# Turning attention probabilities on VectorE and through DRAM instead of on TensorE

## The chip, the cores and the metric

One core of a Trainium2 chip runs the whole kernel. The metric is the device time in microseconds (us), the median of several runs. The engines named below are TensorE (PE), VectorE (DVE), ScalarE (ACT), GpSimd (Pool) and SyncE (SP), which issues most of the transfers; sixteen DMA engines carry them out.

## What is computed

One layer of an encoder block on 512 tokens of width 2048, in float32:

```python
proj = rms_norm(h, g) @ w_in                       # q, k, v of both mixers
att_a = chunk_band_attention(q_a, k_a, v_a, 1, bias_a, sinks)   # 16 heads, 4 key heads, ALiBi
att_b = chunk_band_attention(q_b, k_b, v_b, 8, rel_bias, None)  # 16 heads, relative bias
gates = sigmoid(xn @ w_gate)
h = h + (gates[:D] * (att_a @ w_branch_a) + gates[D:] * (att_b @ w_branch_b)) @ w_out
h = h + square(relu(rms_norm(h, g2) @ w_mlp_in)) @ w_mlp_out
out = rms_norm(h, g3)
```

with, for each head, `p = softmax(q @ k.T / 8 + bias)` and `o = p @ v`. In mixer A a chunk of 64 tokens sees itself and the chunk before it; in mixer B it sees itself and up to eight chunks before it, which for 512 tokens is every chunk up to its own.

## The kernel before

Every product is split into a high and a low part: a matrix is copied by ACT to a float32r tile (`w_hi`, `xn_hi`, `pt_hi`), DVE subtracts that from the original (`w_lo`, `xn_lo`, `pt_lo`), and PE multiplies high by high, high by low and low by high.

The part that matters here is the first stage. It makes 22 blocks of 256 columns (q, k, v and the first gates, `BLOCKS`), each from four units; a unit is a 128 x 1024 piece of weights that SP loads into one of four slots of `landing` (L494), that ACT and DVE split (L686, L1032), and that PE multiplies with 24 matmuls (L1707 to L1709). SP loads unit n when the low part of unit n - 4 is made. There are 88 units, numbered 0 to 87, and the 32 heads of both mixers are hung between them by three lists, written out by hand:

```python
SCORES_AT = [13 + 2 * k for k in range(16)] + [46, 48, 51, 53, 56, 59, 62, 65, 68, 71, 74, 76, 78, 81, 83, 85]
TURN_AT = [n + 1 for n in SCORES_AT]
PV_AT = [n + 2 for n in SCORES_AT]
PV_AT[28] = 81
```

So the scores of a head stand behind unit m on PE (`scores`, L1782), the turning of its probabilities behind unit m + 1 (`turn_probs`, L1796), and the product with the values behind unit m + 2 (`times_v`, L1817). ACT and DVE run the same lists two units later in their own order: in their pass for unit n they handle what hangs on unit n - 2. In such a pass DVE adds the bias and takes the maximum (L1131), splits the unit (L1032), makes the low part of a turned head (L1169), adds up an output (L1145), normalises (L1160), and scales or splits a finished block (L1082 to L1115). ACT splits the unit (L686), copies an output half (L770), takes the exponentials (L751), copies a turned head to `pt_hi` (L761), evacuates a block (L727 to L731 or the gate's sigmoid, L714) and, for the next head, doubles its q (L742, four instructions), for which the next scores wait.

`turn_probs` turns 128 x 128 blocks with a matmul by the identity, from `probs` in SBUF to the PSUM banks that held the scores: 7 blocks for a head of mixer A, 10 for one of B, 272 in all. The scores of the next head therefore wait until DVE has read them.

Beside this, Pool runs `totals` (L1642, L1645): 18 rounds that sum blocks of the two MLP matrices in DRAM for a fast matrix product at the end, each with four copies and four accumulating transfers of 1 MB, DRAM to DRAM, in a chain of waits. Round m starts when PE has used 12 + 8m units (for m up to 9), so round 9 waits for 84 units. Their results are wanted only much later.

Of the kernel before, what the change touches and what calls it, by code (L numbers as in the profile page):

```python
# [13 lines left out]
P = 128  # L14
# [121 lines left out]
def bank_end(h, t):  # L136

    tiles = head_tiles(h)
    return max(i for i in range(TT) if tiles[i][2] == tiles[t][2]) + 1
# [6 lines left out]
def build(nc, x, w_in, a_sinks, b_rel_bias, w_branch_a, w_branch_b, w_gate, w_out,  # L146
          norm_final_g, x_features, norm_gains, identity_in, alibi_in, up_units, x_turned, up_ends, down_blocks, out):
    rel_rows = nc.dram_tensor("rel_rows", (B_HEADS, REL_ROW), F32, kind="Internal").ap()
    h_rows = nc.dram_tensor("h_rows", (SEQ, D), F32, kind="Internal").ap()
    hidden_rows = nc.dram_tensor("hidden_rows", (CHUNKS, 4, P, 4, CB), F32, kind="Internal").ap()  # L150
# [14 lines left out]
    with ExitStack() as ctx:  # L165
# [36 lines left out]

        first_phase = ExitStack()
# [5 lines left out]
        pt_hi = sb("pt_hi", [P, TT, 512], F32R, first_phase)  # L209
        pt_lo = sb("pt_lo", [P, TT, 512], F32R, first_phase)  # L210
# [119 lines left out]
        def turned_part(part, h, t):  # L330

            if h >= A_HEADS:
                return part[:, t, 0:P * (t + 1)]
            if t == 0:
                return part[:, 0:1, 0:P]
            at = 512 * (t - 1) + P
            return part[:].rearrange("p t n -> p (t n)")[:, at:at + 768].rearrange("p (b n) -> p b n", n=384)[:, :, 0:P]
# [58 lines left out]
        pt_done = sem("pt_done")  # L396
# [90 lines left out]
        def _(sp):  # L487
# [32 lines left out]
            for c, (kind, mixer, i) in enumerate(BLOCKS):  # L520
# [4 lines left out]
                for u in range(KU):  # L525
# [26 lines left out]
                    if n - 6 in SCORES_AT and SCORES_AT.index(n - 6) + 2 < HEADS:  # L552
                        strip(SCORES_AT.index(n - 6) + 2)
                    n += 1

# [124 lines left out]
        def _(act):  # L680
# [74 lines left out]
            def turned_probs(h):  # L755
                for t, (first, n, bk, col, _) in enumerate(head_tiles(h)):
                    act.wait_ge(pt_done, TT * h + bank_end(h, t))
                    turned = bank[:, bk, col:col + turned_keys(h, t)]
                    if h < A_HEADS:
                        turned = turned.rearrange("p (b n) -> p b n", n=P)  # L760
                    nc.scalar.activation(turned_part(pt_hi, h, t), turned, ACT.Copy)\  # L761
                        .then_inc(pt_hi_done, 1)
# [10 lines left out]
            def stage(n):  # L773
# [5 lines left out]
                if n in TURN_AT:  # L779
                    turned_probs(TURN_AT.index(n))  # L780
# [22 lines left out]
            for t in range(TT):  # L803
                if t != 2:
                    split(1, (0, 1, None, 2)[t])
                act.wait_ge(rows_landed[t], 16)
                for g in (0, 1):
                    if t >= 2:
                        act.wait_ge(squared, 2 * t + g - 3)
                    nc.scalar.activation(pt_hi[:, (2 * t + g) % 4, :], x_rows[:, t, g * QC:(g + 1) * QC], ACT.Square,  # L810
                                         accum_out=squares[:, t, g:g + 1]).then_inc(squared, 1)
# [207 lines left out]
        def _(dve):  # L1019
# [97 lines left out]
            def biased_scores(h):  # L1117
# [8 lines left out]
                if h:  # L1126
                    dve.wait_ge(pt_done, TT * h)
# [35 lines left out]
            def turned_probs(h):  # L1163
                for t, (first, n, bk, col, _) in enumerate(head_tiles(h)):
                    dve.wait_ge(pt_hi_done, TT * h + bank_end(h, t))
                    turned = bank[:, bk, col:col + turned_keys(h, t)]
                    if h < A_HEADS:
                        turned = turned.rearrange("p (b n) -> p b n", n=P)
                    nc.vector.tensor_tensor(turned_part(pt_lo, h, t), turned, turned_part(pt_hi, h, t).bitcast(F32),  # L1169
                                            ALU.subtract)\  # L1170
                        .then_inc(pt_lo_done, 1)
# [47 lines left out]
            for n in range(2 * KU, UNITS1 + 1):  # L1219
# [7 lines left out]
                if m in TURN_AT:  # L1227
                    turned_probs(TURN_AT.index(m))
# [383 lines left out]
        def _(pool):  # L1612
# [54 lines left out]
            for m in range(2 + STEPS):  # L1667
                pool.wait_ge(unit_used, 12 + 8 * m if m < 10 else 84 + 10 * (m - 9))
# [35 lines left out]
        def _(pe):  # L1704
# [82 lines left out]
            def turn_probs(h):  # L1787
                if h == 0:
                    pe.wait_ge(const_landed, 16)
                    pe.wait_ge(unseen_zero, 1)  # L1790
                for t, (_, n, bk, col, at) in enumerate(head_tiles(h)):
                    pe.wait_ge(probs_ready, TT * h + t + 1)
                    keys = turned_keys(h, t)
                    start = at + n - keys
                    for k in range(keys // P):
                        ins = nc.tensor.transpose(bank[:, bk, col + k * P:col + (k + 1) * P],  # L1796
                                                  probs[:, start + k * P:start + (k + 1) * P], identity[:])
                    ins.then_inc(pt_done, 1)

            def times_v(h):  # L1800
# [5 lines left out]
                pe.wait_ge(pt_lo_done, TT * (h + 1))  # L1806
                if h:
                    pe.wait_ge(att_ready, h)
                for j in range(TT):
# [192 lines left out]
```

## Time and profile before

| | |
|---|---|
| median of 3 runs | 2479.81 us (2479.39 to 2479.84) |
| the profiled execution | 2479.84 us |
| its span in the trace | 2477.9 us |
| PE / DVE / ACT / Pool busy | 99% / 67% / 43% / 8% of the span |
| TensorE clock granted | full, in all 40 slices |
| first stage (units 0 to 87) | to 598.8 us of the span |

The page divides the span into 40 slices of 62 us; slices 2 to 10 are the stage of the change. Matmuls overlap in the records (a 128 x 512 one takes 0.39 us and the next starts 0.23 us after it), so what a piece of PE's work is worth is read from the chain of work that ended last, where overlaps are taken out, and not from the busy time of its group.

### The profile page before, as it was taken

The page shows a single profiled execution, that of the slowest core. Times are in us where ns is not written, and L with a number is a line of the kernel's source. Part 1 is how long each engine was busy: PE and PEld are TensorE (multiplying, and loading weights), DVE is VectorE, ACT ScalarE, POOL GpSimd, SP SyncE. Part 2 cuts the span into 40 slices and gives each one's busy share as a digit, 9 for nine tenths or more (in the row PEclk, how much of TensorE's full clock was granted, in tenths as well). Part 3 has the DMA queues.
Part 4 walks back from the last instruction along what each step waited for, and adds up shares of the span by engine and source line. Part 5 has one row for each costly group of instructions (what it writes and reads, how often), then busy time and mean ns, then how long its engine had stood idle before and what let it go on. Part 6 is the DMA issues. An engine that isn't in the chain of part 4 may idle for free.

```text
span 2477.9 us, 34645 instructions
## 1 busy us (share of the span) xinstructions
PE 2460.3 (99%) x14162; PEld 2176.5 (88%) x14162; DVE 1658.9 (67%) x2252; ACT 1062.5 (43%) x1381; POOL 193.2 (8%) x185
## 2 busy tenths in 40 slices
PE   9999999999999999999999999999999999999998
PEld 8898898898888888888999999999998888888886
DVE  6566555556333332544788888888869788877897
ACT  5566755556222222312433433333335444444445
POOL 0010100100010100001200000000001011110010
PEclk9999999999999999999999999999999999999999
DMA  7789998898889999964564433334478666566652
GB/s 261 208 236 261 240 246 243 233 253 225 227 241 271 245 254 254 251 184 151 167 192 152 136 129 132 133 128 132 133 233 332 232 230 226 190 224 231 233 191 107
DMA packets 226818, 517.10 MB, mean 209 GB/s; under 512 B 30672, under 2 KB 159840, under 8 KB 215152
## 3 DMA queue, kind: packets, MB, share of 16 engines
q1 hardware_dynamic: 213856, 364.04, 44.3%
q0 software_dynamic: 12672, 151.00, 24.1%
q8 instruction: 103, 1.69, 0.3%
q14 instruction: 43, 0.35, 0.0%
q10 hardware_dynamic: 144, 0.02, 0.0%
HBM read 489.80 MB, written 176.20 MB: 269 GB/s over the span
## 4 chain that ended last, share of the span: by engine, by line
PE 96%; DVE 2%; ACT 1%; DMA 0%; issue 0%; SPq 0%; DVEq 0%; ACTq 0%
PE bank L1707 31%; PE bank L1709 31%; PE bank L1708 31%; PE bank L1782 1%; PE bank L1817 1%; PE bank L1796 1%; DMA stream<-in_x_features 0%; DVE up_lo L1398 0%; DVE form_lo_b L1364 0%; DVE at_lo L1248 0%; ACT q_twice L742 0%; DVE ring L1506 0%; ACT w_hi L686 0%; ACT L714 0%; DVE raw_forms L1469 0%
## 5 line engine op out<-in xcount | busy, mean ns | idle before, releaser
L1032 DVE TENSOR_TENSOR w_lo<-landing,w_hi 128x1024 fp32r<-128x1024 f32 x199 | 247.6, 1244 | 447.2 <-ACT w_hi L686 447.1
L1707 PE MATMUL bank<-xn_hi,w_hi 128*128 128x512 f32 x1184 | 464.7, 392 | 2.3 <-DVE w_lo L1189 1.4
L1709 PE MATMUL bank<-xn_hi,w_lo 128*128 128x512 f32 x1184 | 461.2, 390 | 0.0
L1708 PE MATMUL bank<-xn_lo,w_hi 128*128 128x512 f32 x1184 | 460.8, 389 | 0.0
L686 ACT ACTIVATE w_hi<-landing 128x1024 fp32r<-128x1024 f32 x199 | 210.9, 1060 | 575.6 <-PE bank L1709 575.2
L909 ACT ACTIVATE up_hi<-up_raw 128x1792 fp32r<-128x1792 f32 x128 | 218.1, 1704 | 401.8 <-PE bank L1709 395.0
L958 ACT ACTIVATE ring<-down_raw 128x1024 fp32r<-128x1024 f32 x224 | 237.5, 1061 | 312.4 <-PE bank L1709 312.4
L1506 DVE TENSOR_TENSOR ring<-down_raw,ring 128x1024 fp32r<-128x1024 f32 x224 | 284.9, 1281 | 68.3 <-ACT ring L958 68.2
L1398 DVE TENSOR_TENSOR up_lo<-up_raw,up_hi 128x1792 fp32r<-128x1792 f32 x128 | 259.8, 2030 | 85.8 <-ACT up_hi L909 85.8
L1707 PEld LDWEIGHTS bank<-xn_hi,w_hi 128*128 128x128 f32 x1184 | 222.4, 188 | 47.3 <-issue 3.3
L1709 PEld LDWEIGHTS bank<-xn_hi,w_lo 128*128 128x128 f32 x1184 | 222.2, 188 | 46.9
L1708 PEld LDWEIGHTS bank<-xn_lo,w_hi 128*128 128x128 f32 x1184 | 222.5, 188 | 45.0 <-issue 0.2
L1707 PE MATMUL bank<-ring,down_forms 128*128 128x512 f32 x656 | 255.5, 390 | 0.9 <-DVE ring L1506 0.9
L1708 PE MATMUL bank<-ring,down_forms 128*128 128x512 f32 x656 | 255.3, 389 | 0.0
L1709 PE MATMUL bank<-ring,down_forms 128*128 128x512 f32 x656 | 255.2, 389 | 0.0
L1707 PE MATMUL bank<-form_hi_b,up_hi 128*128 128x256 f32 x896 | 253.8, 283 | 0.4 <-DVE up_lo L1398 0.4
L1707 PE MATMUL bank<-form_hi_a,up_hi 128*128 128x256 f32 x896 | 253.6, 283 | 0.0
L1708 PE MATMUL bank<-form_lo_b,up_hi 128*128 128x256 f32 x896 | 253.6, 283 | 0.0
L1709 PE MATMUL bank<-form_hi_b,up_lo 128*128 128x256 f32 x896 | 253.6, 283 | 0.0
L1708 PE MATMUL bank<-form_lo_a,up_hi 128*128 128x256 f32 x896 | 253.6, 283 | 0.0
L1709 PE MATMUL bank<-form_hi_a,up_lo 128*128 128x256 f32 x896 | 253.6, 283 | 0.0
L1707 PEld LDWEIGHTS bank<-form_hi_b,up_hi 128*128 128x128 f32 x896 | 172.0, 192 | 0.7 <-DVE up_lo L1398 0.6
(192 smaller groups left out, 4384.1 us busy)
## 6 DMA issues: line engine op xcount, KB each, us to landing
down_totals<-in_down_blocks POOLq DMA_DIRECT2D x64, 1024.0 KB, 9.5
up_raw<-in_up_units SPq DMA_DIRECT2D x128, 512.0 KB, 3.4
down_raw<-down_totals SPq DMA_DIRECT2D x128, 512.0 KB, 4.4
down_raw<-in_down_blocks SPq DMA_DIRECT2D x96, 512.0 KB, 4.3
landing<-in_w_in SPq DMA_DIRECT2D x71, 512.0 KB, 6.5
landing<-in_w_gate SPq DMA_DIRECT2D x64, 512.0 KB, 6.5
landing<-in_w_out SPq DMA_DIRECT2D x32, 512.0 KB, 3.7
hidden_rows<-hidden_out SPq DMA_DIRECT2D x32, 512.0 KB, 3.3
```

What stands on the lines that cost most here:

```text
L686: nc.scalar.activation(w_hi[:, u % SPLIT, :], landing[:, u % LAND, :], ACT.Copy).then_inc(unit_hi, 1)
L909: nc.scalar.activation(up_hi[n % 2], up_raw[n % 3][:, 1:8, :], ACT.Copy).then_inc(up_hi_done, 1)
L958: nc.scalar.activation(ring[i % RING][:, 0, :], raw_of(i), ACT.Copy).then_inc(piece_hi, 1)
L1032: nc.vector.tensor_tensor(w_lo[:, s, :], landing[:, u % LAND, :], w_hi[:, s, :].bitcast(F32), ALU.subtract).then_inc(unit_lo, 1)
L1398: nc.vector.tensor_tensor(up_lo[n % 2], up_raw[n % 3][:, 1:8, :], up_hi[n % 2].bitcast(F32), ALU.subtract).then_inc(up_lo_done, 1)
L1506: nc.vector.tensor_tensor(part[:, 1, :], raw_of(i), part[:, 0, :].bitcast(F32), ALU.subtract)\
L1707: nc.tensor.matmul(dst, a_hi, b_hi, start=start, stop=False, **kw)
L1708: nc.tensor.matmul(dst, a_hi, b_lo, start=False, stop=False, **kw)
L1709: return nc.tensor.matmul(dst, a_lo, b_hi, start=False, stop=stop, **kw)
L1782: ins = nc.tensor.matmul(bank[:, bk, col:col + n], query[:, t * P:(t + 1) * P], keys[:, first:first + n], start=col == 0 and k == 0, stop= ...
L1796: ins = nc.tensor.transpose(bank[:, bk, col + k * P:col + (k + 1) * P], probs[:, start + k * P:start + (k + 1) * P], identity[:])
L1817: ins = nc.tensor.matmul(dst, v_parts[:, s, j, head, :], moving, start=j == 0 and part is pt_hi, stop=j == TT - 1 and part is pt_lo, skip_ ...
```

## The change

The turning leaves PE. When a head is normalised, DVE turns each of its 128 x 128 blocks in one instruction that transposes the sixteen 32 x 32 blocks each within its own 32 partitions, into a new tile `probs_by_block`. SP stores that tile to DRAM (`turned_probs`, two places in turn) and reads it back with four transfers of 32 partitions each, which put the 32 x 32 blocks on the partitions where they belong (`pt_raw`). ACT and DVE then make `pt_hi` and `pt_lo` from `pt_raw`, each in one instruction per head in place of four. `times_v` reads them in the new order, and for mixer A multiplies whole blocks (256 columns in place of 192). The turned copy is now taken behind unit m + 3 and the values behind unit m + 4. The last head's two are one unit earlier, and its store and loads are issued by Pool, ahead of the wait of round 9. Scores wait for the head before to be biased only.

```diff
-SCORES_AT = [13 + 2 * k for k in range(16)] + [46, 48, 51, 53, 56, 59, 62, 65, 68, 71, 74, 76, 78, 81, 83, 85]
-TURN_AT = [n + 1 for n in SCORES_AT]
-PV_AT = [n + 2 for n in SCORES_AT]
-PV_AT[28] = 81
+SCORES_AT = [13 + 2 * k for k in range(16)] + [46, 48, 51, 53, 56, 59, 62, 65, 68, 71, 74, 76, 78, 80, 82, 84]
+TURN_AT = [n + 3 for n in SCORES_AT[:-1]] + [SCORES_AT[-1] + 2]
+PV_AT = [n + 4 for n in SCORES_AT[:-1]] + [SCORES_AT[-1] + 3]
...
+        def store_probs(queue, h, out):
+            queue.wait_ge(probs_turned, h + 1)
+            if h >= 2:
+                queue.wait_ge(turned_back, 64 * (h - 1))
+            size = turned_size(h)
+            queue.dma_start(turned_probs[h % 2, :, 0:size], probs_by_block[:, 0:size]).then_inc(out, 16)
+        def load_probs(queue, h, out, landed, back):
+            queue.wait_ge(out, landed)
+            if h:
+                queue.wait_ge(pv_done, h)
+            size = turned_size(h)
+            for r in range(4):
+                rows = slice(32 * r, 32 * (r + 1))
+                cols = slice(r * size // 4, (r + 1) * size // 4)
+                src = turned_probs[h % 2, :, cols].rearrange("(a c) n -> c a n", c=32)
+                queue.dma_start(pt_raw[rows, 0:size].rearrange("p (a n) -> p a n", a=4), src)\
+                    .then_inc(back, 16)
...  (SP, behind the load of unit n)
+                    if n - 6 in SCORES_AT:
+                        store_probs(sp, SCORES_AT.index(n - 6), turned_out)
+                    if n - 7 in SCORES_AT:
+                        h = SCORES_AT.index(n - 7)
+                        load_probs(sp, h, turned_out, 16 * (h + 1), turned_back)
...  (DVE)
+            def turn_probs(h):
+                dve.wait_ge(probs_ready, TT * (h + 1))
+                if h == 0:
+                    dve.wait_ge(unseen_zero, 1)
+                else:
+                    dve.wait_ge(turned_out, 16 * h)
+                ...
+                for k, (t, j) in enumerate(blocks):
+                    ...
+                    ins = nc.vector.transpose(out[:, k], probs[:, start:start + P])
+                ins.then_inc(probs_turned, 1)
...
                 if head is not None:
                     normalise(head)
+                    turn_probs(head)
...  (Pool)
             for m in range(2 + STEPS):
+                if m == 9:
+                    store_probs(pool, HEADS - 1, last_out)
+                    load_probs(pool, HEADS - 1, last_out, 16, last_back)
                 pool.wait_ge(unit_used, 12 + 8 * m if m < 10 else 84 + 10 * (m - 9))
...  (PE, scores)
-                    pe.wait_ge(pt_lo_done, TT * h)
+                    pe.wait_ge(biased, TT * h)
```

A head of mixer A moves 128 x 896 floats (0.459 MB) each way, one of B 128 x 1280 (0.655 MB).

## Rows read from the trace of the kernel before

**Rows 1.** The page, part 1: busy time, share of the span, instructions.

```profile
PE 2460.3 (99%) x14162; PEld 2176.5 (88%) x14162; DVE 1658.9 (67%) x2252; ACT 1062.5 (43%) x1381; POOL 193.2 (8%) x185
```

**Rows 2.** Waits of PE from 0 to 1000 us (total, times, longest): the longest.

```profile
PE bank L1707 <- DVE w_lo L1189: 1.4, 1, 1.4
```

**Rows 3.** Chain that ended last, mixer A: start us, us, what.

```profile
94.89 0.77 PE bank L1796 x7
...
101.14 0.84 PE bank L1817 x8
101.98 0.92 PE bank L1782 x8
...
108.38 0.77 PE bank L1796 x7
```

**Rows 4.** The same chain near the end of mixer B.

```profile
561.77 1.19 PE bank L1796 x10
568.42 1.21 PE bank L1817 x8
569.63 1.33 PE bank L1782 x8
```

**Rows 5.** Timeline of DVE, a head of A: start, us, instruction.

```profile
198.83 0.29 DVE L1131 CUSTOM_DVE_ANT_0 probs<-bank,strips 128x128 f32<-128x128 f32 x1 [3.38 <-issue]
...
202.72 0.97 DVE L1160 TENSOR_SCALAR probs<-probs,row_inv 128x128 f32<-128x128 f32 x4
```

**Rows 6.** Timeline of ACT, mixer A: doubling of q, evacuation of a q block.

```profile
206.33 1.27 ACT L742 ACTIVATE q_twice<-q_hi 64x512 fp32r<-64x512 f32 x2
...
220.04 1.92 ACT L731 ACTIVATE q_hi<-side 64x2048 fp32r<-64x2048 f32 x1
```

**Rows 7.** Timelines of DVE and of ACT, a head of B.

```profile
571.10 0.29 DVE L1131 CUSTOM_DVE_ANT_0 probs<-bank,strips 128x128 f32<-128x128 f32 x1 [5.25 <-issue]
...
575.61 1.27 DVE L1160 TENSOR_SCALAR probs<-probs,row_inv 128x128 f32<-128x128 f32 x4
...
575.18 0.19 ACT L751 ACTIVATION_READ_ACCUMULATOR probs<-probs,neg_max 128x1 f32 x1
```

**Rows 8.** Timeline of DVE, a later stage: transposes in blocks of 32 x 32.

```profile
1234.25 1.30 DVE L1344 STREAM_TRANSPOSE mix<-stream 128x512 f32<-128x512 f32 x2
```

**Rows 9.** The page, part 5: splits of 1024 columns on DVE and ACT.

```profile
L1032 DVE TENSOR_TENSOR w_lo<-landing,w_hi 128x1024 fp32r<-128x1024 f32 x199 | 247.6, 1244 | 447.2 <-ACT w_hi L686 447.1
...
L686 ACT ACTIVATE w_hi<-landing 128x1024 fp32r<-128x1024 f32 x199 | 210.9, 1060 | 575.6 <-PE bank L1709 575.2
```

**Rows 10.** Landings of transfers from 90 to 600 us: KB each, median us.

```profile
landing<-in_w_in SPq DMA_DIRECT2D x53, 512.0 KB, 6.4
...
strips<-rel_rows SPq DMA_DIRECT2D x16, 256.0 KB, 7.6
```

**Rows 11.** The same of a later stage: a store to DRAM by 32 partitions.

```profile
h_rows<-turned_ahead SPq DMA_DIRECT2D x24, 128.0 KB, 3.6
```

**Rows 12.** Window: busy PE, PEld, DVE, ACT, POOL, PEclk, DMA share, GB/s.

```profile
78.00:569.00 491.00, 490.37 (x2839) 431.66 (x2838) 288.17 (x719) 303.23 (x629) 49.12 (x73) 1.00 0.90 243
```

**Rows 13.** DMA queues from 78 to 569 us: packets, MB, share of 16 engines.

```profile
q0 software_dynamic: 6334, 75.50, 60.2%
q1 hardware_dynamic: 41850, 43.31, 29.0%
```

**Rows 14.** The same from 0 to 78 us, before Pool moves anything.

```profile
q1 hardware_dynamic: 12352, 17.71, 66.2%
```

**Rows 15.** Waits of Pool from 60 to 600 us for units used by PE.

```profile
POOL down_totals L1642 <- PE bank L1709: 47.8, 8, 8.4
```

**Rows 16.** Timeline of Pool: last transfer of round 8, start of round 9.

```profile
559.46 0.81 POOL L1645 DMA_DIRECT2D down_totals<-in_down_blocks  x1 [4.91 <-DMA down_totals<-down_totals]
568.72 1.02 POOL L1642 DMA_DIRECT2D down_totals<-in_down_blocks  x2 [8.45 <-PE bank L1709]
```

**Rows 17.** Timeline of PE: values of the last head, end of the stage.

```profile
597.56 0.39 PE L1817 MATMUL bank<-pt_hi,v_parts 128*128 128x512 f32 x1
```

More of the change, by code:

```diff
@@ L133, in turned_keys, with turned_blocks @@
     return P * (1 + (t > 0)) if h < A_HEADS else P * (t + 1)
-def bank_end(h, t):
-    tiles = head_tiles(h)
-    return max(i for i in range(TT) if tiles[i][2] == tiles[t][2]) + 1
+def turned_blocks(h):
+    if h < A_HEADS:
+        return [(t, j) for j in range(TT) for t in (j, j + 1) if t < TT]
+    return [(t, j) for j in range(TT) for t in range(j, TT)]
 PV_BANK = 7
@@ L208, in build @@
         v_parts = sb("v_parts", [P, 2, TT, 4, 2 * DH], F32R, first_phase)
-        pt_hi = sb("pt_hi", [P, TT, 512], F32R, first_phase)
-        pt_lo = sb("pt_lo", [P, TT, 512], F32R, first_phase)
+        pt_hi = sb("pt_hi", [P, PROBS], F32R, first_phase)
+        pt_lo = sb("pt_lo", [P, PROBS], F32R, first_phase)
+        probs_by_block = sb("probs_by_block", [P, PROBS], F32, first_phase)
         probs = sb("probs", [P, PROBS], F32, first_phase)
@@ L753, in exponentials, with turned_high @@
                         .then_inc(exp_done, 1)
[L755 to L762, printed above, removed]
+            def turned_high(h):
+                if h < HEADS - 1:
+                    act.wait_ge(turned_back, 64 * (h + 1))
+                else:
+                    act.wait_ge(last_back, 64)
+                size = turned_size(h)
+                nc.scalar.activation(pt_hi[:, 0:size], pt_raw[:, 0:size], ACT.Copy).then_inc(pt_hi_done, 1)
             def attended(h):
@@ L807, in _ @@
                 for g in (0, 1):
-                    if t >= 2:
-                        act.wait_ge(squared, 2 * t + g - 3)
-                    nc.scalar.activation(pt_hi[:, (2 * t + g) % 4, :], x_rows[:, t, g * QC:(g + 1) * QC], ACT.Square,
+                    if t >= 1:
+                        act.wait_ge(squared, 2 * t + g - 1)
+                    nc.scalar.activation(pt_hi[:, g * QC:(g + 1) * QC], x_rows[:, t, g * QC:(g + 1) * QC], ACT.Square,
                                          accum_out=squares[:, t, g:g + 1]).then_inc(squared, 1)
@@ L1161, in normalise, with turned_low @@
                                             ALU.mult).then_inc(probs_ready, 1)
[L1163 to L1171, printed above, removed]
+            def turn_probs(h):
+                dve.wait_ge(probs_ready, TT * (h + 1))
+                if h == 0:
+                    dve.wait_ge(unseen_zero, 1)
+                else:
+                    dve.wait_ge(turned_out, 16 * h)
+                blocks = turned_blocks(h)
+                out = probs_by_block[:, 0:turned_size(h)].rearrange("p (r b j) -> p b r j", r=4, j=32)
+                for k, (t, j) in enumerate(blocks):
+                    _, n, _, _, at = head_tiles(h)[t]
+                    start = at + n - turned_keys(h, t) + P * (j if h >= A_HEADS else j - max(t - 1, 0))
+                    ins = nc.vector.transpose(out[:, k], probs[:, start:start + P])
+                ins.then_inc(probs_turned, 1)
+            def turned_low(h):
+                dve.wait_ge(pt_hi_done, h + 1)
+                size = turned_size(h)
+                nc.vector.tensor_tensor(pt_lo[:, 0:size], pt_raw[:, 0:size], pt_hi[:, 0:size].bitcast(F32),
+                                        ALU.subtract).then_inc(pt_lo_done, 1)
             nc.vector.memset(ones, 1.0).then_inc(ones_ready, 1)
@@ L1785, in scores @@
                 ins.then_inc(scores_done, 1)
[L1787 to L1798, printed above, removed]
             def times_v(h):
```

45 lines of the change are left out of this document (25 added, 20 removed).

## The prediction

> **What bounds the kernel now.** I read the page first: PE is busy 99% of the span [rows 1]. Then the waits of PE: over the first 1000 us, where the whole change lies, the longest is 1.4 us [rows 2] and all five kinds together are 5.2 us. So nothing but PE's own work sets the time, and any instruction taken from PE is worth its full length as long as nothing becomes late. The next question is what has room. DVE is busy 288 of 491 us in the stage of the change, ACT 303, but the DMA engines 0.90 of the time [rows 12]. That is the resource to watch: the queues' table gives 60.2% of the sixteen engines to Pool's sums in DRAM and 29.0% to SP's loads [rows 13]. Pool waits for PE only 47.8 us in eight rounds [rows 15], 6 us a round; the rest of the time it is in its chain of transfers.
>
> **What PE loses.** In the chain that ended last the seven turnings of a head of A are 0.77 us, the ten of one of B 1.19 us [rows 3, 4]. 16 x 0.77 + 16 x 1.19 = 31.4 us go. `times_v` of A has 256 columns in place of 192 in six of eight matmuls; in B eight matmuls with 512 to 128 columns take 1.21 us, in A eight of 192 and 128 take 0.84 [rows 3, 4], so it grows by well under 0.1 a head; I take 0.5 us in all. The moving operand is now read in runs of 32 elements. No row shows such a read; bounds are nothing and a doubling of `times_v` (16 x 0.84 + 16 x 1.21 = 33 us). I take nothing, since B's reads in runs of 128 columns cost 1.21 us for 2560 columns, 0.47 ns each, against 5.48 us for the 12288 of a unit, 0.45 ns each. That the scores now wait for `biased` alone gains nothing, as PE did not wait there. The sum without new waits: 2479.8 - 31.4 + 0.5 = 2449 us.
>
> **What DVE and ACT get.** Two transposes of 128 x 512 take 1.30 us [rows 8], 0.16 us per 128 columns if only columns count; the smallest DVE instruction of 128 columns takes 0.29 [rows 5]. I take 0.29: 2.0 us for a head of A, 2.9 for B, 79 us in all, so DVE goes to about 75% of the stage. `pt_hi` and `pt_lo` become one instruction each, by the 1024-column rows [rows 9] 0.93 and 1.09 us in A (896 columns), 1.3 and 1.55 in B (1280), somewhat less than before. Queued behind the turning on DVE is the split of the next unit. In A normalising ends 4.9 us after the scores [rows 5], the turning 6.9; with a q block's scaling (2.8 us) the split would end at 10.9, and PE wants it 11.0 after (two units of 5.5, from the end of one turning to the next values [rows 3]). Its cover is just enough; if it is gone it costs tenths, in some six places.
>
> **What the transfers cost one by one.** A load of 512 KB takes 6.4 us in this stage, one of 256 KB 7.6 [rows 10]; the nearest store, in a quieter stage, 3.6 [rows 11]. Store and read-back follow each other, and the four reads are issued one after another (about 0.5 us each, 1.5 more). So D, from the turning's end to the data back, is 6.4 + 1.5 + 6.4 = 14.3 us, with bounds 8.7 (3.6 twice) and 16.7 (7.6 twice). Three places want it sooner:
> - In B, nine heads have the next scores three units on. There DVE's and ACT's passes take the bias and exponentials of head h + 1 ahead of the turned copy of head h. A loop closes: turning of h, D, `pt_hi` 1.3, `pt_lo` 1.55, normalising h + 1 (1.27 and 0.2), turning h + 1 (2.9): 7.2 + D = 21.5, against a period of 3 x 5.5 + 1.21 + 1.33 = 19.0 [rows 4]. 2.5 x 9 = 23 us. Even with D short, the exponentials end 4.3 us after the scores of h + 1 [rows 7], then come 1.3 and 1.55: 7.2 against one unit of 5.5, so 1.6 x 9 = 14 us at least.
> - In A, ACT must copy the head, often evacuate a block (1.92) and double q (2 x 1.27) [rows 6] before the scores after next: 6.9 + 14.3 + 0.93 + 1.92 + 2.54 = 26.6 against 2 x (11.0 + 0.84 + 0.92) - 0.92 = 24.6: 2 us for each of the eight heads with an evacuation, 16 us.
> - The last heads of B, two units apart: 5.8 + 2.9 + 14.3 + 2.9 = 25.9 against 24.5, of which each head bears half: 4 us.
> Together some 43 us, which alone would give 2449 + 43 = 2492. SP is blocked meanwhile at its read-back, for the store and for the values of the head before; queued behind it are the loads of units, which have four units (22 us) of lead and cover it. DVE's own new wait, for the store of the head before, has 12.7 us in A and more in B, against one landing of 6.4 to 7.6; behind it stands the split of the next unit. Behind ACT's wait for the read-back stand the evacuation and the doubling priced above.
>
> **What the transfers cost together.** This decides. Up to the last head Pool has to finish rounds 0 to 8, for the last head's store stands on Pool's queue in front of round 9, behind a 1 MB transfer of round 8. Before, that transfer was issued at 559.5 and Pool then waited until 568.7 [rows 16]. The engines' time up to there, from 78 us on: 0.602 x 491 = 296 us for Pool, 0.290 x 491 = 142 for SP, 2 for the rest, 440 of 491. The 31 heads before the last add 2 x (16 x 0.459 + 15 x 0.655) = 34.3 MB. One MB of SP's queue takes 142 / 43.31 = 3.3 us beside Pool, and alone 0.662 x 78 / 17.71 = 2.9 us [rows 13, 14]: 100 to 113 us more. I take 100, since packets are longer in the stores. No row excludes that part of it fits between Pool's packets; the bound on that side is nothing. 440 + 100 = 540 us of work at a share of 0.975 are 554 us: the last transfer of round 8 ends at 78 + 554 = 632 us, where PE, 31 us ahead, wants the last head at 567. Then come its store (2 to 3 us behind the queue), the issue of the reads by Pool and their landing (about 5.5), `pt_hi`, `pt_lo` (2.9): 643 us, against 597.6 before [rows 17]. That is 45 us later: 2525 us. The waits of the 43 us above lie within this, as PE would only come earlier to the same stop. Since at the end of the stage the queues empty while PE stands, I take some of it back and forecast 2520. Queued on Pool behind the last head's waits is round 9 and all after it; Pool has time for them, as rounds 10 on have ten units each.
>
> The Trainium skill, "DMA: Bandwidth & Descriptors", section "Where 436 GB/s comes from", says otherwise: HBM to SBUF transfers are bound by 358 GB/s of HBM per core, with 435 of the fabric above it. The window shows 243 GB/s at 0.90 [rows 12], which does not bear that out for this mix. By the page there would be room for the added 74 GB/s, no late Pool, and the kernel would end on the faster side. Its fit in "Anatomy of one DMA" (an estimate by that page: 2.0 us and bytes by 436 GB/s) would make D 6 to 7 us, against the 6.4 of one landing here.
>
> **Rivals.**
> 1. The DMA engines have room, and D is short, 9 us or less. For it: SP's queue alone moved 17.71 MB in 0.662 x 78 us of engine time, 343 GB/s [rows 14], well over the 243 of the stage. Against: the tenth that is idle is about the 6 us in each round of some 55 that Pool pauses [rows 15], so with Pool at work hardly any of it is free. Then 2449 plus a few us where the loop in B does not fit: 2449 to 2463. The point from which it decides is added DMA work under 50 us, the idle tenth of 491.
> 2. Pool keeps up enough and the latencies alone set it: 2492.
> 3. Starved queue: SP's transfers share badly with Pool's long packets. If D is 20, the loop in B is 27.2 against 19.0 (74 us), A 7.7 x 8 = 62, the end 18: 2449 + 154 = 2603.
> 4. It does not do what it says, as the strided read of PE or DVE's lateness takes back the 31 us: about 2480.
>
> **How the numbers follow.** Late Pool 0.55 (2500 to 2560 by 90 to 113 us and a share of 1.0 to 0.95), rival 1 0.17, rival 2 0.16, rival 3 0.07, rival 4 0.05. What a measurement can tell from no change is about 0.2%, 5 us. Faster 0.17, same 0.06, slower 0.77. The forecast's own range is 2496 to 2560; the range that holds 8 in 10 reaches into the faster case, 2453 to 2570.
>
> **What would show it.** In the profile after: DMA share near 1.0 from 90 us on; Pool's waits for PE gone in the rounds up to 8 and its chain some 65 us a round; the last head's store issued after 600 us; PE waiting once for tens of us at the values of the last head (L1817's successor) for `pt_lo`; a few us per head in B. Wrong it would be if the longest wait of PE is short and the DMA share stays at 0.90.

## The result and the profile after

| | before | after |
|---|---|---|
| median | 2479.62 us (2479.39 to 2479.84) | 2578.44 us (2576.74 to 2589.19) |
| ratio | | 1.0407 [1.0393, 1.0421] |
| profiled execution, span | 2479.84, 2477.9 us | 2589.19, 2587.3 us |
| end of the first stage | 598.8 us | 706.5 us |

The change makes the kernel 99 us slower. The measured time lies outside the predicted range of 2453 to 2570 us. Almost the whole difference arises in the first stage: it ends 107.7 us later, of 109.4 us in the spans. The profiled execution is the slowest of its four, so its balance comes to 109 us.

The page after, part 1 (busy time, share of the span, instructions; compare [rows 1]) and part 4 (the chain that ended last, by engine):

```profile
PE 2469.9 (95%) x13890; PEld 2176.0 (84%) x13890; DVE 1709.4 (66%) x2428; ACT 1052.0 (41%) x1283; POOL 195.8 (8%) x190
...
PE 87%; DMA 5%; issue 3%; DVE 2%; ACT 2%; SPq 1%; POOL 0%; DVEq 0%; ACTq 0%; POOLq 0%
```

The 272 turnings are gone (14162 - 13890 matmuls), and yet PE is busy for 10 us more. Without them it should be busy 2460.3 - 31.4 + 0.5 = 2429.4 us, so 40.5 us have been added to the work that stayed. Idle it is 2587.3 - 2469.9 = 117.4 us against 17.6. The balance: 31 us are saved, 100 us of waits and 40 us of slower work are added, together 109. Waits and slower work are both seen in the window of the stage (columns as in [rows 12]) and in PE's waits from 60 to 760 us (total, times, longest):

```profile
78.00:569.00 491.00, 418.33 (x2148) 359.19 (x2147) 276.31 (x736) 247.98 (x460) 41.15 (x61) 0.92 0.93 256
```

```profile
PE bank L1858 <- issue: 72.7, 22, 14.8
PE bank L1837 <- ACT q_twice L781: 17.9, 11, 2.7
PE bank L1858 <- DVE stream L1184: 7.1, 1, 7.1
PE bank L1858 <- DVE pt_lo L1221: 2.8, 1, 2.8
```

L1858 is `times_v`, L1837 `scores`. In the same stretch before, the longest kind of wait was 0.6 us in all. PE now waits 24 times ahead of the values of a head, once 14.8 us and otherwise up to 9. And TensorE's granted clock is 0.92 in place of 1.00: after such waits PE works at the lower of its levels, 1.2 in place of 2.4 GHz. The chain that ended last shows one whole turn of this, a head of A (start us, us, what):

```profile
300.09 1.48 DVE probs_by_block L1214 x7
301.59 8.38 DMA turned_probs<-probs_by_block
309.99 0.33 SPq L364
310.36 0.43 SPq L364
310.83 0.43 SPq L364
311.31 8.18 DMA pt_raw<-turned_probs
319.53 0.94 issue
...
323.49 0.63 ACT q_twice L781
324.13 0.63 ACT q_twice L781
324.77 0.64 ACT q_twice L781
325.54 2.00 PE bank L1837 x8
...
331.00 0.42 PE bank L1764
331.42 0.24 PE bank L1762
...
341.19 0.92 PE bank L1837 x8
```

From the turning's end to the data back are 17.9 us: 8.4 for the store, 1.3 for SP's issues, 8.2 for the last of the four reads. The prediction calls this time D. Read in the same way for each of the 31 heads whose transfers SP issues, D is 18.6 us on average (19.4 in A, 17.8 in B, from 9 to 32): 0.4 until SP issues the store, 7.9 for the store, 0.5 until SP issues the first read, 2.3 between the first and the fourth issue, 7.5 for the fourth read. Then ACT copies the head, evacuates a block and doubles q, and only then can PE make scores. They take 2.00 us and a matmul 0.42 (the lower level); 6 us after PE has restarted, a matmul takes 0.24 again, and the next scores 0.92. Landings from 78 to 600 us (KB each, median us; compare [rows 10]):

```profile
landing<-in_w_in SPq DMA_DIRECT2D x55, 512.0 KB, 8.3
turned_probs<-probs_by_block SPq DMA_DIRECT2D x16, 448.0 KB, 6.8
pt_raw<-turned_probs SPq DMA_DIRECT2D x64, 112.0 KB, 7.8
turned_probs<-probs_by_block SPq DMA_DIRECT2D x10, 640.0 KB, 8.8
pt_raw<-turned_probs SPq DMA_DIRECT2D x40, 160.0 KB, 6.2
```

SP's waits from 60 to 720 us; it stands for the turning (L352), for the values of the head before, whose `pt_lo` lies in the memory that the read-back overwrites (L358), and for the store to land (L364):

```profile
SPq L352 <- DVE probs_by_block L1214: 107.7, 27, 10.5
SPq L358 <- PE bank L1858: 95.9, 21, 10.4
SPq L364 <- DMA turned_probs<-probs_by_block: 83.1, 20, 10.4
```

These sums look larger than what they cost the trip. SP's wait for the values runs beside the store's way to DRAM, and the read is issued on average 0.5 us after the store has landed. Nor does SP's standing starve anybody else here. From 60 to 720 us the longest waits of ACT are these, and neither in its list nor in DVE's is there a wait for a load of weights or for a bias strip; every strip has landed 14.7 us or more before DVE takes it:

```profile
ACT w_hi L725 <- PE bank L1764: 138.5, 55, 5.3
ACT pt_hi L801 <- DMA pt_raw<-turned_probs: 99.5, 21, 16.9
```

And Pool's waits from 78 to 720 us, against [rows 15]:

```profile
POOL down_totals L1694 <- PE bank L1764: 101.3, 7, 30.5
...
POOL turned_probs L352 <- DVE probs_by_block L1214: 36.8, 1, 36.8
```

Pool waits for PE twice as long as before and stands 36.8 us for the last head's turning. It is not late.

### The profile page after: what moved, and what is told of

The parts are those of the page before. It is cut to its first block, busy times and chain, and to the rows that moved or that the text cites. A ratio compares the mean times of both kernels' runs of the same rounds, so it can differ in the third digit from the quotient of the medians.

```text
span 2587.3 us, 34432 instructions
## 1 busy us (share of the span) xinstructions
PE 2469.9 (95%) x13890; PEld 2176.0 (84%) x13890; DVE 1709.4 (66%) x2428; ACT 1052.0 (41%) x1283; POOL 195.8 (8%) x190
## 4 chain that ended last, share of the span: by engine, by line
PE 87%; DMA 5%; issue 3%; DVE 2%; ACT 2%; SPq 1%; POOL 0%; DVEq 0%; ACTq 0%; POOLq 0%
PE bank L1762 28%; PE bank L1763 28%; PE bank L1764 28%; DMA pt_raw<-turned_probs 2%; DMA turned_probs<-probs_by_block 2%; PE bank L1858 1%; PE bank L1837 1%; ACT q_twice L781 1%; SPq L364 1%; DMA stream<-in_x_features 0%; DVE up_lo L1450 0%; DVE form_lo_b L1416 0%; ACT probs L790 0%; DVE probs_by_block L1214 0%; DVE probs L1170 0%
## 5 line engine op out<-in xcount | busy, mean ns | idle before, releaser
L1763 PE MATMUL bank<-xn_lo,w_hi 128*128 128x512 f32 x1184 | 466.0, 394 | 0.0
```

Of the source, the lines that this page charges most:

```text
L1763: nc.tensor.matmul(dst, a_hi, b_lo, start=False, stop=False, **kw)
```

## The experiments

Theory, as the profile after suggests it: the trip through DRAM takes as long as the four units given to it or longer, because its two transfers land in 6 to 9 us each beside Pool's sums, and a closed loop (values, SP, read-back, copies, values) hands every microsecond of it to PE. Rivals: the order of DVE's and ACT's passes; the added bytes; SP's queue; PE's clock. The column "waits" is PE's, all kinds, from 60 to 760 us; clock, DMA share and rate are those of 78 to 569 us. e3 and e4 are one run each, e2, e7, e9 to e12 and e14 two.

| | us | waits | clock | DMA share, GB/s |
|---|---|---|---|---|
| before | 2479.6 | 0.8 | 1.00 | 0.90, 243 |
| after | 2578.4 | 100.5 | 0.92 | 0.93, 256 |
| e1 no trip | 2485.0 | 27.5 | 0.99 | 0.90, 242 |
| e2 traffic only | 2532.9 | 38.9 | 0.97 | 0.94, 261 |
| e3 quiet Pool | 2492.2 | 34.2 | 0.99 | 0.61, 174 |
| e4 filler | 2586.7 | 33.8 | 0.98 | 0.95, 260 |
| e5 loose traffic | 2480.3 | 0.8 | 1.00 | 1.00, 278 |
| e6 no trip, pass order | 2472.0 | 16.1 | 0.99 | 0.91, 246 |
| e9 after, pass order | 2597.0 | 99.9 | 0.91 | 0.93, 257 |
| e10 and own buffer | 2598.6 | 103.7 | 0.91 | 0.93, 255 |
| e11 and one unit later | 2551.3 | 70.8 | 0.94 | 0.98, 272 |
| e12 and two units later | 2538.3 | 58.0 | 0.95 | 1.01, 281 |
| e13 as e12, quiet Pool | 2482.8 | 22.5 | 0.99 | 0.61, 176 |
| e14 after, one unit later | 2571.1 | 92.2 | 0.92 | 0.94, 263 |

**e1, the change without its transfers.** DVE turns, ACT and DVE copy from a standing tile in place of the turned head (so the output is another), and nothing goes to DRAM.

```diff
 def store_probs(queue, h, out): 
+    return
 def load_probs(queue, h, out, landed, back):
+    return
-    act.wait_ge(turned_back, 64 * (h + 1))
+    act.wait_ge(probs_turned, h + 1)
```

> The changed kernel with neither the store nor the read-back of any head: ACT and DVE make pt_hi and pt_lo of the same size from a standing tile (so the values multiply a fixed piece of the normalised input and the output is another), still behind the turning on DVE. All else stays: turning on DVE, order of 32 x 32 runs for PE, the later places. Theory 1 (the round trip through DRAM is what PE waits for, and its waits also lower the clock): all of the loss goes, 2449 to 2460 us, waits of PE in the stage under 10 us in all, clock 1.0. Rival (the turning on DVE, the order of its passes in the nine gaps of three units, or the short runs that PE reads are what costs): well above, 2480 us or more. The late copies in the gaps of three units alone would be 14 us of it.

2484.98 us, ratio 1.0023 [1.0012, 1.0035]. So the trip costs 93 of the 99 us. But the time is the rival's, 2480 or more: the 31 us that PE is spared are lost before any transfer is added: PE waits 27.5 us, most of it in thirteen waits of at most 1.7 us ahead of the values. The time is 36 us above the 2449 of the sum, 8.5 more than these waits:

```profile
PE bank L1854 <- issue: 18.6, 13, 1.7
PE bank L1833 <- ACT q_twice L779: 5.6, 5, 2.1
```

**e2, the traffic without the change.** The kernel before, where SP stores as much from another tile and reads it back into unused columns, at the places of the change on SP's queue, for 22 heads; nobody uses the data. The waits differ from those of the change: the store waits for the exponentials instead of the turning, and the read for the read before instead of the values.

```diff
+if n - 6 in SCORES_AT and SCORES_AT.index(n - 6) < 22:
+    store_probs(sp, SCORES_AT.index(n - 6))    # waits for probs_ready
+if n - 7 in SCORES_AT and SCORES_AT.index(n - 7) < 22:
+    load_probs(sp, SCORES_AT.index(n - 7))     # waits for the store
```

> The kernel before, with the store and the four reads of the first 22 heads issued by SP at the places of the change, with the same sizes and packets, from a standing tile into a tile that nobody reads; no compute engine waits for them. Theory 1 (latency): 2480 us within 3, as nothing waits; the landings of SP's loads rise from 6.4 to about 8 us. Rival 2 (the sixteen DMA engines are full, so that the added bytes cost time by themselves, through late loads of weights or a late Pool): 10 us slower or more.

2532.94 us, 1.0216 [1.0186, 1.0246]. SP's wait for the stores to land is what hurts. Behind it on SP's queue stand the bias strips and the weights, and here DVE and ACT do wait for them (60 to 720 us):

```profile
SPq L360 <- DMA turned_probs<-xn_hi: 188.5, 22, 15.6
...
DVE probs L1161 <- DMA strips<-in_alibi: 69.7, 8, 15.2
...
ACT w_hi L716 <- DMA landing<-in_w_in: 84.5, 18, 11.4
```

PE waits 27.2 us ahead of its turnings for `probs` and 10.5 for q. These 53 us are not a price that can be put into the change. Here `probs` is ready when SP comes to it, so the store is issued right behind a strip and a unit's load (0.04 us after the last of them, in the change 2.9 us) and 448 KB land in 12.1 us, in the change in 6.8. SP stands 188.5 us for 22 stores here, in the change 83.1 us for 31.

**e5, the same bytes, loosely.** As e2, but the read-back stands two units later on SP's queue and four places in DRAM take turns, so that SP finds the store landed.

```diff
-if n - 7 in SCORES_AT and SCORES_AT.index(n - 7) < 22:
-    load_probs(sp, SCORES_AT.index(n - 7))
+if n - 9 in SCORES_AT and SCORES_AT.index(n - 9) < 22:
+    load_probs(sp, SCORES_AT.index(n - 9))
```

> As the run with the traffic alone, but the read-back of a head is issued two units later, behind the next head's store, and there are four places in DRAM, so that SP does not stand at the store's landing before it issues biases and weights. Same bytes, same packets. Theory 1b (it was SP's in-order queue: 188 us of waits for the stores' landings held back strips and weights): 2480 to 2490 us. Rival (the bytes themselves cost it, the engines being full at 0.94): 2525 us or more.

2480.32 us, 1.0004 [0.9994, 1.0015]. The window (columns as in [rows 12]):

```profile
78.00:569.00 491.00, 490.36 (x2837) 431.31 (x2836) 288.14 (x719) 302.95 (x629) 46.01 (x68) 1.00 1.00 278
```

PE is as full as before while the DMA engines go from 0.90 to 1.00. A unit's weights land in 12.0 us in place of 6.4, and PE does not wait, because they have 22 us. So for these 22 heads the bytes cost PE nothing. What costs is a landing that somebody waits for. Pool does fall behind: its last transfer of round 8 (compare [rows 16]: 559.46, then a wait of 8.45 for PE) and the start of round 9 are

```profile
597.50 0.81 POOL L1680 DMA_DIRECT2D down_totals<-in_down_blocks  x1 [6.59 <-DMA down_totals<-down_totals]
598.03 1.30 POOL L1677 DMA_DIRECT2D down_totals<-in_down_blocks  x2
```

38 us later and with no wait for PE. In e5 PE does not need Pool by then.

**e3, a quiet Pool.** Pool's copies and sums of rounds 0 to 8 are cut to 16 of their 128 rows, an eighth (128 KB in place of 1024), and most readers of the sums take the raw blocks (the output is another).

```diff
 def copied(src, dst):            # and added() alike
+    if m < 9:
+        src, dst = src[0:16], dst[0:16]
```

> The changed kernel with Pool's sums of rounds 0 to 8 cut to an eighth of their size (16 of 128 partitions), their readers pointed at the raw blocks instead, so that the output is another. The DMA engines are then about half idle in the stage. Theory 1 with latencies set by the crowd on the engines: store and read-back fall from some 7 to 9 us each to 3.5 to 5, the waits of PE from 100 us to under 30, the time to 2465 to 2500 us. If the latencies are fixed costs or SP's own queue instead: no lower than 2550 us.

2492.18 us (one run), 86 below the change. Landings:

```profile
landing<-in_w_in SPq DMA_DIRECT2D x55, 512.0 KB, 3.8
turned_probs<-probs_by_block SPq DMA_DIRECT2D x16, 448.0 KB, 2.5
pt_raw<-turned_probs SPq DMA_DIRECT2D x64, 112.0 KB, 2.6
```

With 2.5 and 2.6 us in place of 6.8 and 7.8 the trip fits, and what is left is e1's 27 us and 6.8 us at the last head. D is 10.0 us on average in place of 18.6. The trip is dear because of what it shares the engines with.

**e4, filler.** Twelve matmuls of 512 columns, whose results nobody uses, ahead of PE's wait for `pt_lo` at every head.

```diff
+for _ in range(12):
+    nc.tensor.matmul(bank[:, PV_BANK, :], xn_hi[:, 0, 0:P], xn_hi[:, 1, :], start=True, stop=True)
 pe.wait_ge(pt_lo_done, h + 1)
```

> The changed kernel with 12 more matmuls of 128 x 512 (2.7 us at the full clock) on PE ahead of each head's wait for pt_lo, into the bank that the values then overwrite. They sit in time in which PE waits anyway for most heads. Theory 1 (each wait of PE also brings slow matmuls behind it, 39 us in all by the stage's mean clock of 0.92): the clock of the stage rises above 0.97 and the time falls, by 10 to 40 us. Rival (the slow clock costs nothing, as the round trip is the loop that closes): same time or up to 20 us more, whatever the clock.

2586.68 us (one run; the change's four lie between 2576.7 and 2589.2). The waits fall from 100 to 34 us and the clock of the window rises from 0.92 to 0.98, and the time doesn't fall. The filler is 32 x 2.7 = 88 us more work for PE, and the kernel is at most 10 us longer: PE has that much room, and what sets the pace of a head is the trip. What the slow clock costs by itself e4 can't say, since the filler takes the place of what it saves; the slow scores (2.00 us) of the turn shown above do stand in the chain that ended last. The Trainium skill, "TensorE: Matmul & The Clock Gate", section "HAM oscillation — how this bites in real kernels", describes this pattern (PE waits for a transfer, restarts at the lower clock, again and again); the trace after agrees, with matmuls of 0.42 us and then 0.24. That a warm PE gains something here, e4 does not show.

**e6, pass order without the trip.** ACT and DVE make an earlier head's turned copies ahead of the next head's exponentials and bias, and q's doubling goes ahead of the evacuation of gates or values.

```diff
-if n in SCORES_AT:
-    exponentials(SCORES_AT.index(n))
-if n in TURN_AT:
+if n in TURN_AT and n in SCORES_AT:
     turned_high(TURN_AT.index(n))
+if n in SCORES_AT:
+    exponentials(SCORES_AT.index(n))
```

> The run without the trip (2485 us), with three changes of order: in the gaps of three units ACT makes pt_hi ahead of the next head's exponentials and DVE pt_lo ahead of its biases, and ACT doubles q ahead of evacuating a gate or v block. Theory 2 (27 us of PE's waits there and the clock behind them are the order of the passes): 2449 to 2462 us. Rival (turning on DVE or PE's short runs cost it): 2480 us or more.

2471.99 us, 0.9967 [0.9954, 0.9981]: 13 of the 36 us between e1 and the 2449 of the sum come back, 23 do not. The time lies between the theory's range and the rival's. Even with a free trip, then, this change in this order is worth some 8 us.

**e7 and e8, Pool's sums later.** Rounds 0 to 8 wait for unit 88 on; e8 has the pass order too, and the last head's data come back into a buffer of their own.

```diff
-    pool.wait_ge(unit_used, 12 + 8 * m if m < 10 else 84 + 10 * (m - 9))
+for m in range(9):
+    pool.wait_ge(unit_used, 88 + 9 * m)
```

> The changed kernel, complete, with Pool's rounds all behind the first stage: rounds 0 to 8 while PE does units 88 to 160 and rounds 9 to 17 in the MLP's first product. Store and read-back then have the engines nearly to themselves. Theory 1 (crowding by Pool's sums is most of the loss): as with the sums cut down, 2485 to 2500 us. If the moved sums are too late for their readers: over 2520 us, with waits of PE behind 1200 us.

> The changed kernel, complete, with Pool's rounds behind the first stage, the three changes of order, and the last head read back into the tile probs, so that its loads do not wait for the values of the head before. Sum of theories 1 and 2: 2455 to 2468 us, under the kernel before. If one of the two is wrong: 2480 us or more.

2620.57 us, 1.0567 [1.0546, 1.0589], and 2602.53, 1.051 [1.048, 1.0539]: the rival of "over 2520" came, and neither theory. The first stage is as good as hoped (e8: PE busy 475.0 of 491 us with the trip, as in e6 without it). The loss moves to the MLP, where the rounds now run: PE's longest kind of wait from 760 us on in e7 (before, all kinds together were 1.3 us there):

```profile
PE bank L1764 <- DVE up_lo L1450: 85.6, 29, 7.1
```

Behind it are slow loads more than late sums: DVE waits 134.5 us for pieces of the MLP matrix (before, 1.3), which land in 5.6 us in place of 3.4, and ACT 22.9 us for sums. The stretch to which the rounds were moved is no empty one; another was not tried.

**e9 and e10, the parts that might close the loop.** e9 is the change with e6's pass order; e10 adds a place of its own for the data read back, so that SP need not wait for the values of the head before.

```diff
-            if h:
-                queue.wait_ge(pv_done, h)
+            if h and h < 22:
+                queue.wait_ge(pt_lo_done, h)    # data go to unused columns of `stream`
```

> The changed kernel with the other pass orders of e6 alone (turned copies of an earlier head ahead of the next head's exponentials and bias, q's doubling ahead of an evacuation where that block is a gate or values). Theory: pass order was worth 13 us without the trip (2485 to 2472), and with the trip it also moves ACT's standing at the read-back ahead of the exponentials, so it can cost as well as give; 2565 to 2580, with pt_lo's waits of PE still over 70 us. Rival, that the loss of the changed kernel is pass order and the trip merely lies in it: below 2520.

> e9 and a place of its own for the data read back: for heads 0 to 21 the unused columns of feature blocks 11 to 13, for the last head the scores' buffer, so that SP doesn't stand until the values of the head before are done (95.9 us of SP's waits in the changed kernel). Theory that the single buffer closes the loop values, SP, read-back, pt_lo, values: SP's wait goes, the read starts 2 to 4 us earlier, PE's waits fall by half: about 2530. Rival, that the landings of 7 to 8 us each way set it, whatever SP waits for: within 10 us of e9.

2597.0 us, 1.0473 [1.0443, 1.0503], and 2598.6, 1.0479 [1.0449, 1.051]. Neither gains anything. The order, if anything, costs (19 us against the change's median, 8 against its slowest execution); a likely reason, not tested by itself, is that ACT stands at the read-back (130.0 us in place of 99.5) with the exponentials behind it. In e10 SP's wait for the values and for `pt_lo` is 61.7 us where e9's for the values was 91.1, its wait for the store grows in turn (92.1 to 107.5), and PE waits as long as before. The wait for the values had run beside the store's landing, so that removing it brings the read no earlier. By itself the buffer repairs nothing; of the two outcomes expected for e10 the rival came.

**e14, e11 and e12, lead.** e14 is the change with the turned copies and values of heads 0 to 27 one unit later, nothing else; e11 is the same on top of e10; e12 has two units more than e10 (heads 0 to 25) and the read-back one unit later on SP's queue.

```diff
-TURN_AT = [n + 3 for n in SCORES_AT[:-1]] + [SCORES_AT[-1] + 2]
-PV_AT = [n + 4 for n in SCORES_AT[:-1]] + [SCORES_AT[-1] + 3]
+TURN_AT = [n + 4 for n in SCORES_AT[:28]] + [n + 3 for n in SCORES_AT[28:-1]] + [SCORES_AT[-1] + 2]
+PV_AT = [n + 5 for n in SCORES_AT[:28]] + [n + 4 for n in SCORES_AT[28:-1]] + [SCORES_AT[-1] + 3]
```

> e10 with the turned copies and the values one unit later (four and five units after the scores) for heads 0 to 27; the store and the read stay where they are on SP. Theory: the trip needs store 7, SP's turn, read 8 and two passes, 19 us after the turning, against some 15 given; one unit is 5.5 us more, so PE's waits for pt_lo nearly go and the time is 2480 to 2500, the same bytes moving. Rival, that SP standing at the store's landing (83 us) starves the loads of weights and bias strips: waits move to the issue of the weights' split or to the bias, and the time stays above 2520.

> e10 with the read-back one unit later on SP and the turned copies and the values two units later (five and six after the scores) for heads 0 to 25. Now SP need not stand at the store's landing either. Theory, that SP's order and the closeness of the steps are the whole cause and the bytes cost nothing (e5, 2480 with the turning by PE left in): PE has no waits of note before the last heads, and the time is that of e6, 2472, and up to 2485 with the last six heads still tight. Rival, that at a DMA share of 1.00 the units' loads or the last head's store come late: over 2500.

> The changed kernel with one edit: turned copies and values of heads 0 to 27 one unit later. Theory, that lead is what was short and the single buffer and the pass orders do not matter: 2545 to 2560, as e11. Rival, that the single buffer matters once the lead is there, since the read of a head stands behind the values of the head before, and these are now later as well: 2575 or more, no better than the changed kernel.

e14 2571.1 us, 1.037 [1.0325, 1.0415]; e11 2551.3, 1.0289 [1.0259, 1.0319]; e12 2538.3, 1.0237 [1.0207, 1.0266]. Lead, the number of units between a head's scores and its values, was short: on top of e10, one unit is worth 47 us. By itself it is worth only 7 (e14's two runs, 2566 and 2576, against the change's 2577 to 2589). What holds it back in e14 is seen on SP, which stands for the values of the head before (60 to 720 us):

```profile
SPq L358 <- PE bank L1858: 214.2, 30, 14.6
```

Within D, SP's standing is now 3.8 us a head, in the change 0.9, in e11 1.0. So the buffer matters once the lead is there. How much is not shown: e11 has e6's pass order too, which e14 lacks, and lead with that order but without the buffer was not run. Against the change e11 gains 27 us. e12's second unit, with the later read-back, gives only 13 more. My expectations for e11 and e12 were too low by some 50 to 70 us, and e14 came out between its theory and its rival, nearer to the rival. In e12 SP's wait for the store has gone from 107.5 to 17.9 us, the engines are as full as in e5, and PE still waits 58 us:

```profile
78.00:569.00 491.00, 454.35 (x2438) 395.27 (x2437) 307.20 (x816) 273.30 (x502) 45.23 (x67) 0.95 1.01 281
...
PE bank L1872 <- issue: 27.6, 12, 4.1
PE bank L1872 <- DVE stream L1196: 15.7, 2, 10.1
```

**e13, e12 with a quiet Pool.** e3's edit on top of e12: an eighth of the rows, not the sixteenth that the expectation says, with the readers of the sums pointed at the raw blocks.

> e12 with Pool's copies and sums of rounds 0 to 8 cut to a sixteenth of their rows, so the down product's sums are wrong and nothing else changes. Theory, that what is left of e12's loss is transfers made slow by Pool's: 2472 to 2482, as e6. Rival, that it is the short lead of the last six heads, which no unit can be found for: above 2500, with waits of PE after 550 us alone.

2482.75 us, 1.0015 [1.0003, 1.0026], a hair above the theory's range. The short lead of the last heads still costs its 10 us (two waits), and all waits together are 22.5 us. Of e12's 66 us above e6, 56 are landings beside Pool's sums: stores take 7.6 us in A and 9.7 in B, and with the quiet Pool 2.7 and 3.2.

Pool at work or quiet gives 2578 and 2492 at the change's lead, 2538 and 2483 at e12's. Late landings thus cost 86 us at the one lead and 56 at the other; more lead takes 40 us off while Pool works, and 9 otherwise, with all that e12 has besides. No version here beats the kernel before and still turns the probabilities; e6 does, by 8 us and without its transfers.

## Why the prediction was wrong

- **What bounds the kernel, and PE's 31 us: right.** The turnings are gone. The bound for the strided read (nothing to 33 us) is settled at its lower end: two 256-column matmuls that read runs of 32 start 0.12 us apart, just as the columns want, and at the full clock `times_v` takes 0.88 us in A and 1.23 in B (0.84 and 1.21 before). The value taken was right.
- **DVE: right in sign, too dear.** Seven transposes take 1.48 us (the chain above), 0.21 each in place of 0.29, so 56.5 us in all and not 79. It explains none of the miss.
- **Pass order, "14 us at least" in B: right, but not all of it.** e1, without a transfer, has nine waits of 1.4 to 1.7 us ahead of the values between 349 and 538 us, 14.7 us in all. The other 13 us of its waits, mostly in A and 7.9 us of them for q, and the 8.5 us by which it is slower beyond its waits have no term in the sum.
- **D: mechanism right, size wrong; this term failed.** The sum took 14.3 us (6.4 + 1.5 + 6.4) and bounded it by 8.7 and 16.7. It measured 18.6 on average, above the upper bound: 7.9 for the store, 7.5 for the fourth read, 2.3 instead of 1.5 for the issues, and 0.9 of SP's standing that had no term. With 19.4 in A and 17.8 in B the prediction's own three places give (7.2 + 17.8 - 19.0) x 9 = 54 in B, (31.7 - 24.6) x 8 = 57 in A and some 14 at the end (an estimate between the sum's 4 and rival 3's 18), 125 in place of 43: 2449 + 125 = 2574 us, where 2578 was measured. That it comes so close is partly luck. The trace has 100 us of waits, at 24 heads and not only in the three places, and the rest is slower work, for which the sum has no term.
- **SP "covered by four units of lead": this step held.** In the change neither ACT nor DVE waits for a load of weights or a strip. e2 shows what it looks like when it does not hold: 53 us with the turning left on PE, and e5 takes it all back by issuing the read later, with four places in DRAM.
- **"What the transfers cost together. This decides": the premise failed, and it was the step that the forecast stood on.** It let PE keep its pace up to the last head, had Pool finish round 8 at 632, and booked one stop of 45 us there. After the change PE falls back at 24 heads, the rounds that follow its units fall back with it, and Pool, far from late, waited 101 us for PE and 37 for the last head. For what it was made for, Pool's lateness, the arithmetic on the DMA engines comes out in e5, whose 22 heads add 22.5 MB: the same steps give 440 + 22.5 x (100 / 34.3) = 506 us of work, at 0.975 an end at 78 + 519 = 597 us, and the last transfer is issued at 597.50. Two small errors cancel in it, as the share was 0.99 up to there and the work so 514 us. But the late transfer was not what PE waited for. I had a full resource show itself as one late transfer at the end, and it showed itself first as landings of 6 to 9 us in a loop that is passed 31 times. That the forecast of 2520 has the right sign is luck in its mechanism: one large term, which never came, stands in the place of another.
- **PE's clock: missing.** No step reckoned with it. In the balance it is 40 us. e4, with a faster clock and more work, is no faster; how much of the 40 us the trip would have taken anyway stays open.
- **Rival 1 (room on the engines, 2449 to 2463): half true.** There is room for the bytes of 22 heads (e5), but landings beside Pool's sums are slow, and D was not short. The Trainium skill, "DMA: Bandwidth & Descriptors", section "Where 436 GB/s comes from", puts the limit of HBM to SBUF transfers at 358 GB/s for a core. The most that a window here shows is 281 GB/s at a share of 1.01, with Pool's DRAM to DRAM sums among it. The prediction took such a gap as evidence against the figure; no run here is evidence for or against it. The profile's page before has 666.0 MB read and written in HBM where the DMA engines moved 517.1, so the rates of the windows lie below those at the HBM. (The 74 GB/s that the prediction adds should be 70: 34.3 MB in 491 us.)
- **Rival 2 (latencies alone, 2492)** was right in kind: Pool keeps up and the latencies set the time. Its number lacks the measured D. That e3 comes to 2492 too is chance, as its D is 10.0 us.
- **Rival 3 (D = 20, 2603)** was nearest in mechanism: transfers of SP that share badly with Pool's. Its D is the nearest to 18.6, and its time is nearer to the measured one than the forecast; I gave it 0.07.
- **What would show it.** Of the signs named, the DMA share near 1.0, the vanished waits of Pool and the single long stop are all absent. The last head's store was issued after 600 us (687), for another reason: all of PE was late. The sign said to refute the forecast, a longest wait that is short (14.8 us, and else under 9) with a DMA share that stays near 0.90 (0.93), is what came.

What stays open: what the slow clock costs by itself, how much of e11's gain is the buffer and how much the pass order, and where the 7 us go by which e6 lies above 2449 beyond its 16 us of waits. A trip for the sixteen heads of A alone was not tried.

## What to carry to other kernels

Price a store and read-back by their landings under the load that will be there, twice, and count to the last of several reads; add each in-order wait of the queue that issues them, and then ask whether a loop closes over them. Here, where a consumer waited for the data, an idle tenth of the DMA engines helped nothing; where no one waited (e5), even a share of 1.00 cost nothing. Lead without a second buffer lengthens the hold of the first (e14), and a buffer without lead leaves the consumer as early as it was (e10). A long wait of an issuing queue may cost nothing when it runs beside a transfer that is in flight anyway. And before a gain on the bound engine is booked, run the new order of the other engines without the new cost: here (e1) all 31 us were gone already.

## What the runs showed of the hardware

- Transfers beside Pool's sums take 2.2 to 3 times as long to land: 448 KB stored in 6.8 us and in 2.5, reads of 112 KB in 7.8 and in 2.6, 512 KB loaded in 8.3 and in 3.8 (change and e3), at DMA shares of 0.93 and 0.61.
- The same store of 448 KB takes 12.1 us to land when it is issued right behind a strip and a load of 512 KB on the same queue (e2), and 6.8 us when it is issued 2.9 us behind them (change), at shares of 0.94 and 0.93.
- The DMA engines go to a share of 1.00 and 278 GB/s without a wait of PE, when nobody waits for the added bytes and the weights, which land in 12.0 us, have 22 us (e5).
- With waits at 24 heads PE's granted clock averages 0.92 over the stage. Behind the wait before 325.5 us there are 6 us of work at the lower level (1.2 GHz), behind the one before 372.4 us 3; a matmul of 512 columns then takes 0.43 us in place of 0.23.
- VectorE transposes 128 x 128 in float32, as sixteen 32 x 32 blocks, every 0.21 us (seven in 1.48 us).
